# Up projection of a transformer block as seven products of quarters instead of eight, on one Trainium2 core

## What is computed

```python
xn2 = rmsnorm(x, norm2_g[l])
x = x + jnp.square(jax.nn.relu(xn2 @ w_up[l])) @ w_down[l]
```

## Time and profile before

| | |
|---|---|
| median of 3 runs | 1969.29 us |
| span of the profiled execution | 1967.4 us, 1.9 us less than the median |
| TensorE busy | 1959.2 us (100%), 9686 matmuls |
| VectorE busy | 1024.1 us (52%) |
| ScalarE busy | 764.9 us (39%) |
| GpSimd busy | 83.8 us, all after 1806 us |
| DMA | 183.36 MB, mean 93 GB/s, from the queues of SyncE and ScalarE |

### The profile page before, as it was taken

How to read it: one execution, slowest core, us unless ns; L and a number is a source line. 1 busy time by engine, 2 the same in 40 slices (tenths; PEclk the granted TensorE clock), 3 DMA queues, 4 the chain that set the end, 5 groups by cost and what they waited for, 6 DMA issues and landing times.

```text
span 1967.4 us, 23153 instructions
## 1 busy us (share of the span) xinstructions
PE 1959.2 (100%) x9686; PEld 1614.8 (82%) x9686; DVE 1024.1 (52%) x1394; ACT 764.9 (39%) x1226; POOL 83.8 (4%) x132
## 2 busy tenths in 40 slices
PE   9999999999999999999999999999999999999998
PEld 8888888888888888888888888888888888887776
DVE  5553466435453436643334355545554447596675
ACT  5556563332323333442134232222222321447864
POOL 0000000000000000000000000000000000005541
PEclk9999999999999999999999999999999999999999
DMA  6222222223122242233233323232323334521011
GB/s 214 84 68 85 65 86 75 86 91 106 65 91 86 87 148 86 86 107 108 86 105 89 106 86 107 86 107 89 105 86 107 86 124 114 152 81 44 23 55 65
DMA packets 184295, 183.36 MB, mean 93 GB/s; under 512 B 5120, under 2 KB 159232, under 8 KB 184192
## 3 DMA queue, kind: packets, MB, share of 16 engines
q1 hardware_dynamic: 179840, 172.15, 28.2%
q10 hardware_dynamic: 4352, 9.75, 1.6%
HBM read 175.59 MB, written 4.19 MB: 91 GB/s over the span
## 4 chain that ended last, share of the span: by engine, by line
PE 98%; ACT 1%; DVE 0%; DMA 0%; issue 0%; POOL 0%; DVEq 0%; ACTq 0%
PE bank L1403 85%; PE bank L1630 2%; PE bank L1611 2%; PE bank L1644 2%; PE bank L1501 1%; PE bank L1490 1%; PE bank L1529 1%; PE bank L1413 1%; ACT raw L1663 0%; PE bank L1464 0%; PE bank L1433 0%; PE bank L1509 0%; PE bank L1577 0%; PE bank L1446 0%; PE bank L1620 0%; PE bank L1431 0%
## 5 line engine op out<-in xcount | busy, mean ns | idle before, releaser
L1403 PE MATMUL bank<-xh,wh 128*128 128x512 f32 x1352 | 534.1, 395 | 0.0
L1403 PE MATMUL bank<-xh,wl 128*128 128x512 f32 x1352 | 527.6, 390 | 0.0
L1403 PE MATMUL bank<-xl,wh 128*128 128x512 f32 x1352 | 527.0, 390 | 0.0
L1680 ACT CAST wh<-raw 128x2048 fp32r<-128x2048 f32 (+2 forms) x151 | 279.5, 1854 | 408.8 <-PE bank L1403 405.1
L2234 DVE TENSOR_TENSOR wl<-raw,wh 128x2048 fp32r<-128x2048 f32 (+2 forms) x151 | 335.0, 2221 | 169.5 <-ACT wh L1680 169.3
L1403 PEld LDWEIGHTS bank<-xh,wl 128*128 128x128 f32 x1352 | 253.4, 187 | 53.8
L1403 PEld LDWEIGHTS bank<-xh,wh 128*128 128x128 f32 x1352 | 253.7, 188 | 50.3
L1403 PEld LDWEIGHTS bank<-xl,wh 128*128 128x128 f32 x1352 | 253.8, 188 | 50.0
L1403 PE MATMUL bank<-wh,xh 128*128 128x512 f32 x320 | 129.4, 404 | 0.0
L1403 PE MATMUL bank<-wh,xl 128*128 128x512 f32 x320 | 125.1, 391 | 0.0
L1403 PE MATMUL bank<-wl,xh 128*128 128x512 f32 x320 | 125.1, 391 | 0.0
(11 more groups left out here) (325 smaller groups left out, 2925.8 us busy)
## 6 DMA issues: line engine op xcount, KB each, us to landing
raw<-in_w_in SPq DMA_DIRECT2D x49, 1024.0 KB, 5.0
raw<-in_a_w_in SPq DMA_DIRECT2D x32, 1024.0 KB, 5.5
raw<-in_w_up SPq DMA_DIRECT2D x16, 1024.0 KB, 5.3
raw<-in_w_down SPq DMA_DIRECT2D x16, 1024.0 KB, 5.8
raw<-in_w_proj_b SPq DMA_DIRECT2D x8, 1024.0 KB, 5.1
raw<-in_a_w_out SPq DMA_DIRECT2D x8, 1024.0 KB, 5.7
raw<-in_w_out SPq DMA_DIRECT2D x4, 1024.0 KB, 5.2
raw<-in_w_kv SPq DMA_DIRECT2D x4, 1024.0 KB, 4.9
```

Source lines behind the costliest of these rows:

```text
L1403: m = e.matmul(o, p, q, start=k == 0 and n == 0, stop=k == K - 1 and n == 2)
L1680: m = e.copy(hi, r)
```

## The change

A group g of 512 columns of `w_up` within a half f is cut into quarters A, B, C and D of 512 x 256 (rows 0 to 511 are A and B, rows 512 to 1023 C and D; A and C are the first 256 columns). The tokens are cut into two times 256. In place of the eight products of quarters, seven are made, each of a sum of weights with a sum of x: A, A+B, A+B+D, A+B+D+C, B+D, C and D. One product is 24 matmuls with 256 columns moving (`seven`, three terms, two column blocks t, four k). There are 28 a half, in the sequence `SEVENS`, as pairs of group and number.

- Four of a group's products (1, 6, 5, 3) are accumulated into one bank. Three snapshots of it are copied to SBUF by ScalarE (`shot`, after 1, 6 and 5); the next product into the bank waits for the snapshot. Products 2, and 7 with 4, have banks of their own. VectorE adds or subtracts bank and snapshot and then applies maximum and `rs` (`piece`), piece 12 without the first step. ScalarE squares and rounds, VectorE makes the low part (`piece_low`, placed behind the next product).
- Each product has its own half slot (128 x 1024) of `wh`, `wl`, of which there are four; `part` splits the weights of the product four places on, on ScalarE and VectorE. In the list it stands behind the piece of the product that frees the slot.
- SyncE loads quarters of 512 KB into six half slots of `raw`. A+B is added in SBUF by VectorE (`add_weights`). A+B+D, A+B+D+C and B+D are made by DMAs issued from GpSimd that add a quarter from memory to the slot (`sum_weights`), after the low part of the product before is made.
- The sums of x (differences of the token halves and of the row halves) are made after each tile of `wo` by VectorE, in `between`, with high and low parts in `xh`, `xl` and new tiles `xeh`, `xel` of 768 columns a row.
- `ROOT[1]` is 2: the sum of squares and root come after the third product. `("up", 0, 2)` is no longer split in four pieces. Some semaphores are merged, `yh`, `yl` and others have new places in SBUF, a wait of `pa_low` is gone, and the indices of the splits in the last stretch are renumbered.

```diff
+SEVENS = [(0, 1), (1, 1), (0, 2), (0, 7), (0, 6), (1, 2), (0, 5), (1, 7), (0, 3), (0, 4),
+          (1, 6), (2, 1), (1, 5), (2, 2), (2, 7), (1, 3), (1, 4),
+          (2, 6), (3, 1), (2, 5), (3, 2), (3, 7), (3, 6), (2, 3), (3, 5), (2, 4), (3, 3), (3, 4)]
+SUM_OF = {1: ("A", 0), 7: ("A", 1), 6: ("A", 2), 3: ("A", 3), 5: ("B", 1), 2: ("C", 0), 4: ("D", 0)}
+PRODUCT_OF = {x: n for n, x in SUM_OF.items()}
+ADDED = {("A", 1): "B", ("A", 2): "D", ("A", 3): "C", ("B", 1): "D"}
+INTO = {1: "12", 6: "12", 5: "12", 3: "12", 2: "11", 7: "21", 4: "21"}
+SHOT = {1: "11", 6: "21", 5: "22"}
+X_PART = {1: 0, 5: 1, 2: 2, 3: 3, 7: 4, 6: 5, 4: 6}
+PIECE_OF = {2: "11", 5: "22", 3: "12", 4: "21"}
...
-            for j in range(2):
-                col(("up", f, c, j), ("up", f, c), j * 128, 8, ("x", 1), "out_d")
+        for x, g in QUARTER_LOADS:
+            chunk(("quarter", f, g, x), "w_up", 512 * (x in "CD"), 4, f * 2048 + g * 512 + 256 * (x in "BD"), 256,
+                  "quarter")
+        SPLIT.extend(("seven", f, g, n) for g, n in SEVENS)
...
+for _n, _c in enumerate(SPLIT):
+    _wide = 1 if _c[0] == "seven" else 2
+    WSLOT[_c] = _next // 2 if _wide == 2 else _next
+    _old = {_held[_next + x] for x in range(_wide)} - {None}
+    for x in range(_wide):
+        _held[_next + x] = _c
+    _next = (_next + _wide) % 4
+    if _old:
+        BEFORE[_c] = sorted(_old, key=SPLIT.index)
+        AFTER.setdefault(BEFORE[_c][-1], []).append(_c)
...
+def sum_ready(g, x, step):
+
+    at = SEVENS.index
+    return at((g, 5)) - 7 if x == "B" else at((g, PRODUCT_OF[x, step - 1])) - 3
+
+
+def sevens(f):
+
+    line = SEVENS
+    sums = sorted((sum_ready(g, x, step), g, x, step) for g in range(4) for x, step in ADDED if (x, step) != ("A", 1))
+    out, low = [], []
+    for i, (g, n) in enumerate(line):
+        while sums and (sums[0][0] <= i or i == len(line) - 1):
+            out.append(("sum_weights", f, *sums.pop(0)[1:]))
+        out.append(("seven", f, g, n))
+        if f == 0 and i == ROOT[1]:
+            out += [("sum_squares", 1), ("root", 1)]
+        if n in SHOT:
+            out.append(("shot", f, g, n))
+        if n in PIECE_OF:
+            out.append(("piece", f, g, PIECE_OF[n]))
+        out += low
+        for t in after_chunk(("seven", f, g, n)):
+            out += [t] + ([("add_weights", *t[1:3])] if t[0] == "part" and t[3] == 1 else [])
+        low = [("piece_low", f, g, PIECE_OF[n])] if n in PIECE_OF else []
+    return out + low
 
 
...
-        o += whole(("up", 1, 0, 0), ("up", 1, 0, 1)) if f else rooted(1, ("up", 0, 0, 0), ("up", 0, 0, 1))
-        o += whole(*[("up", f, c, j) for c in range(8) for j in range(2)][2:])
+        o += sevens(f)
...
+        def seven(f, g, n):
+            into = INTO[n]
+            if n in (1, 2, 7):
+                take("st" + into, ("st", f, g, into), ("st_out", f, g, into))
+            elif n == 4:
+                w.wait_ge(*told("st_out", f, g, "22"))
+            else:
+                w.wait_ge(*told("shot", f, g, {6: 1, 5: 6, 3: 5}[n]))
+            bank = bank_of("st" + into, ("st", f, g, into))
+            w.wait_ge(*told("lo", ("seven", f, g, n)))
+            hi, lo = split_half(("seven", f, g, n))
+            for t in range(2):
+                for k in range(4):
+                    w.wait_ge(*(told("xl", 1, k + 4, "sums") if X_PART[n] > 3 else told("xl", 1, k + 4 * (X_PART[n] > 1))))
+                    c = slice(k * 256 + t * 128, k * 256 + t * 128 + 128)
+                    h, l = x_sum(n, k)
+                    for x, (p, q) in enumerate(((hi, h), (hi, l), (lo, h))):
+                        m = e.matmul(bank[:, t * 256:(t + 1) * 256], p[:, c], q,
+                                     start=n in (1, 2, 7) and t == 0 and k == 0 and x == 0,
+                                     stop=t == 1 and k == 3 and x == 2, skip_group_check=True)
+            m.then_inc(*tell("tile", ("seven", f, g, n)))
+
...
+        def part(f, g, n):
+            name, (x, step) = ("seven", f, g, n), SUM_OF[n]
+            if (x, step) == ("A", 1):
+                w.wait_ge(*told("lo", "added", f, g))
+            elif step:
+                w.wait_ge(*told(f"sum{SUMS.index((f, g, x, step)) % 3}", f, g, x, step))
+            else:
+                w.wait_ge(*told(f"half{SLOT[PLACE['quarter', f, g, x]]}", f, g, x))
+            for old in BEFORE[name]:
+                w.wait_ge(*told(*chunk_read(old)))
+            e.copy(split_half(name)[0], raw_half(("quarter", f, g, x))).then_inc(*tell("hi", name))
+
+        def shot(f, g, n):
+            piece = SHOT[n]
+            w.wait_ge(*told("tile", ("seven", f, g, n)))
+            if piece_before(f, g, piece):
+                w.wait_ge(*told("hl", *piece_before(f, g, piece)))
+            elif piece == "11":
+                w.wait_ge(*told("xl", 1, 6 + g, "sums"))
+                w.wait_ge(*told("xl", 1, 6 + g))
+            elif piece == "21":
+                w.wait_ge(*told("sum_square", 1, 7))
+            else:
+                w.wait_ge(*told("ssq", 1))
+            e.copy(shot_place(g, piece)[:, :], bank_of("st12", ("st", f, g, "12"))[:, :]).then_inc(*tell("shot", f, g, n))
+
+        def piece(f, g, c):
+            t = shot_place(g, c)
+            w.wait_ge(*(told("st_out", f, g, c) if c == "12" else told("st_out", f, g, c, "relu")))
+            act(t[:, :], t[:, :], ACT.Square).then_inc(*tell("up_sq", f, g, c))
+            if f:
+                w.wait_ge(*told("tile", ("down", 0, 7, 0)))
+            else:
+                after("mix")
+            w.wait_ge(*told("up_sq", f, g, c))
+            e.copy(h_part(hh, g, c), two(t[:, :])).then_inc(*tell("hh", f, g, c))
...
         def wo(c, j):
-            gain(1, c * 2 + j, ("gb", 3, 1))
...
+            k = c * 2 + j
+            t, v = tmp[2 + k % 3], between[:, k % 2, :]
+            w.wait_ge(*told("tile", ("gb", 3, 1)))
+            w.wait_ge(*told("gain", 1, k))
+            if k < 4:
+                e.copy(xh[:, 2 * k, 0:256], t[:, 0:256]).then_inc(*tell("xh", 1, k))
+                w.wait_ge(*told("x_sum", k))
+                e.copy(xh[:, 2 * k, 256:512], v[:, 0:256]).then_inc(*tell("xh", 1, k, "sums"))
+            else:
+                e.copy(xh[:, 2 * k - 7, :], t[:, :]).then_inc(*tell("xh", 1, k))
+                w.wait_ge(*told("x_sum", k))
+                e.copy(xeh[:, k - 4, :], v[:, 0:768]).then_inc(*tell("xh", 1, k, "sums"))
...
+            if s == 1:
+                t, v = tmp[2 + k % 3], between[:, k % 2, :]
+                w.wait_ge(*told("xh", 1, k))
+                if k < 4:
+                    e.tensor_tensor(xl[:, 2 * k, 0:256], t[:, 0:256], xh[:, 2 * k, 0:256], ALU.subtract)
+                    w.wait_ge(*told("xh", 1, k, "sums"))
+                    e.tensor_tensor(xl[:, 2 * k, 256:512], v[:, 0:256], xh[:, 2 * k, 256:512], ALU.subtract).then_inc(
+                        *tell("xl", 1, k))
+                else:
+                    e.tensor_tensor(xl[:, 2 * k - 7, :], t[:, :], xh[:, 2 * k - 7, :], ALU.subtract).then_inc(*tell("xl", 1, k))
+                    w.wait_ge(*told("xh", 1, k, "sums"))
+                    e.tensor_tensor(xel[:, k - 4, :], v[:, 0:768], xeh[:, k - 4, :], ALU.subtract).then_inc(*tell("xl", 1, k, "sums"))
+                return
...
-            add_x(("wo", c, j), c * 2 + j, 1, "norm2_g")
+            k = c * 2 + j
+            t, v = tmp[2 + k % 3], between[:, k % 2, :]
+            add_x(("wo", c, j), k, 1, "norm2_g")
+            w.wait_ge(*told("gain", 1, k))
+            if k >= 2:
+                w.wait_ge(*(told("xl", 1, k - 2, "sums") if k >= 6 else told("xl", 1, k - 2)))
+            if k < 4:
+                e.tensor_tensor(v[:, 0:256], t[:, 0:256], t[:, 256:512], ALU.subtract).then_inc(*tell("x_sum", k))
+                if k == 0:
+                    e.tensor_scalar(minus_g, v_("norm2_g")[:, 0:4], -1.0, None, ALU.mult).then_inc(*tell("x_sum", "minus"))
+                return
+            stt(v[:, 0:256], xT[:, k - 4, 256:512], v_("norm2_g", k - 4), t[:, 256:512], ALU.mult, ALU.subtract).then_inc(
+                *tell("x_sum", k, "x_less"))
+            w.wait_ge(*told("x_sum", k, "x_less"))
+            w.wait_ge(*told("x_sum", "minus"))
+            stt(v[:, 256:512], xT[:, k - 4, 0:256], minus_g[:, k - 4:k - 3], v[:, 0:256], ALU.mult, ALU.add).then_inc(
+                *tell("x_sum", k, "x_least"))
+            w.wait_ge(*told("x_sum", k, "x_least"))
+            e.tensor_tensor(v[:, 512:768], t[:, 0:256], v[:, 256:512], ALU.add).then_inc(*tell("x_sum", k))
...
+        def part(f, g, n):
+            name = "seven", f, g, n
+            w.wait_ge(*told("hi", name))
+            hi, lo = split_half(name)
+            e.tensor_tensor(lo, raw_half(("quarter", f, g, SUM_OF[n][0])), hi, ALU.subtract).then_inc(*tell("lo", name))
+
+        def add_weights(f, g):
+            first, second = ("quarter", f, g, "A"), ("quarter", f, g, "B")
```

(41 more changed lines are left out.)

298 lines of the change are left out of this document (169 added, 129 removed).

## The result

The kernel after takes 2032.83 us (median of 4 runs, 2032.22 to 2034.21), the kernel before 1969.45 us beside it: a ratio of 1.0323, with a 95% interval of 1.0308 to 1.0337. That is 63.4 us slower. The forecast was 2021 us, 51.7 us slower, with a range of 1996 to 2056 us.

A forecast was written before the change was run, and what follows sets the result against it. TensorE bounds the kernel before; after, the VectorE-ScalarE chain was to limit the up stages. The four feed-forward stages were summed to 400 against 348.4 us, 51.5 more, added to the 1969.3 median: 2021 us, range 1996 to 2056.

The forecast's parts named there:

- The exchange of VectorE and ScalarE: Up stages: 4.83 us per piece with a part behind it, 24.8 us per group where TensorE needs 19.8.
- The sums: GpSimd's accumulating DMAs in the up stages: 7 us landing, each us lost four times, two places per half.
- TensorE's own work: Up stages: 174.2 us of products removed, 158.6 us of quarter products added; 15.6 us less if nothing else limited.
- Start and ends: Up stages: a 7.6 us stand at the first start; at each end the down split holds TensorE 3.8 us.
- The clock, taken at 0: TensorE's stands could lower its clock to 1.2 GHz: bounds 0 and 22 us, taken as 0.
- "Edits at no cost": Whole change: renamed and merged semaphores, missing pa_low wait, moved tiles, snapshots and load slots were said to cost nothing.
- nowhere else: Expected sign: TensorE waits some 50 us in the two up stages, for wl and the snapshot, and in no other place.
- Rival 1: Up stages: TensorE still limits, only the 15.6 us saving remains, 1954 us; chance 0.08.
- Rivals 2 and 3: Sums land in 3.4 us or less, 2006 us, chance 0.18; or take 10 to 12 us, chance 0.19.
- Rival 3: Up stages: sums take 10 to 12 us, by GpSimd's issue or DMA load, 2040 to 2060 us; chance 0.19.

The follow-up runs named there:

- fill: The kernel after with unread 128x256 matmuls put into TensorE's stands in the up stages, computation untouched: 2035.97 us (1.0337).
- best2: The kernel after with part rounding ahead of ScalarE's square and copy, another product order and banks moved back by two: 1969.10 us (0.9999).

## Why the prediction was right, and where it was off

The direction and the mechanism held: forecast 2021, measured 2032.8 us, 11.8 us more. Some 6 of these are the bank rotation and 5.4 the four stages. In part the nearness is luck: a sum was put at 7 us and lands in 6.0, which made the forecast 4 us too long and hid as much of what was put too short. With 6.0 the same sum of terms gives 2017. By its own steps:

- **The exchange of VectorE and ScalarE.** Right, and confirmed by taking it away (38.3 us). A piece with a part behind it takes 4.86 us for 4.83. The group of seven was put at 24.8 us; in after, products 5 of groups 1 and 2 are 26.2 us apart, in fill 24.8 in the first half and 25.8 in the second. TensorE's waits in the two up stages and at their ends add up to 48.4 us, for some 50.
- **The sums.** Landing 6.0 us (5.8 to 10.6) where 7 was taken; ScalarE stands 7.3, 7.5, 7.5 and 5.5 us in the four places, for about 8.2, and 2.1 in a fifth, behind a sum that took 8.0 us to land. Four places, 3.5 to 3.7 us per us of landing for 4. The reason given for 7, that the destination is read too and so the time doubles, was wrong in its size: the addition costs 1.7 us, and a plain load takes 4.3 from GpSimd and 3.8 from SP.
- **TensorE's own work.** The row gave 0.1175 us per matmul from four of them; in a full stage they start 0.12 apart, 80.6 us per half for 79.3. Of 174.2 us then 12.9 are saved and not 15.6, and best2's second half shows 4.5 of its 6.4.
- **Start and ends.** A stand of 8.6 us before the third product, for 7.6, ended by the low part of its weights in VectorE's late queue. Up stages of 121.6 and 106.9 us for 119.3 and 105.6, down stages of 88.1 and 88.8 for 87.5. In the last, nine of the first matmuls start late by 1.7 us in all, behind the stand at the hand-over.
- **The clock, taken at 0.** TensorE's clock did fall, in ten places of the two up stages, the granted mean being 0.90 and 0.92. The forecast's stages, 399.9 us, are 5.4 short of the 405.3; the 1.3 us of a group and the 1.7 us of the last stage fit the clock, but fill, with most of the slow matmuls gone, left the up stages as long as they were. What makes these 5 us stays open.
- **"Edits at no cost".** This is the step that failed. The list had renamed semaphores, moved tiles and slots. It did not have the ring of PSUM banks, from which the up stages no longer take 32 tiles. It costs 5.9 us, outside the two stages, where "nowhere else" had been written.
- **The rivals.** Rival 1 (TensorE limits, 1954) is what best2 comes near to in its second half; it needed another order on ScalarE, as its condition said, and still gained nothing in the whole: of the 4.5 us of the second half, 3.0 go in the first up stage, 1.0 in the down stage behind it and 0.8 ahead of the stages. Rivals 2 and 3 fell by the landing of 6.0 us. Rival 3's landings of 10 us exist, for the second of two sums in a row (9.8 to 10.6 us), but ScalarE stands for none of these in after. The load on the DMA engines, 0.64 of the time in a stage and 0.84 in best2's, did not keep best2's second half from its 82.4 us.

## What to carry to other kernels

When a change takes tiles out of a rotation (banks, slots, buffers), list every rotation by its count modulo its length, because all that comes later shifts; a shift shows as a new wait far from the edit, and moving the rotation on in the old kernel tests it in one run. When two in-order engines hand work to each other, put first on each queue what the other one waits for: here that alone was worth 38 us, more than the matrix work saved. A sum by DMA wants other products between the part that it waits for and the part that waits for it: one more product there cut ScalarE's waits from 29.9 to 4.8 us.

## What the runs showed of the hardware

An accumulating DMA of 512 KB from GpSimd lands in 6.0 us, the same without the addition in 4.3, one of 32 KB, accumulating, in 2.8; they hold GpSimd's queue for 1.28, 0.75 and 0.85 us. Of two accumulating ones in a row the second takes 9.8 to 10.6 us. VectorE and GpSimd, both on SBUF, stretch each other: 0.68 to 1.22 us and 0.49 to 1.04 us on VectorE, 0.72 to 1.22 on GpSimd. The Trainium skill, page "SBUF — State Buffer", section "Who interferes with whom", says that a VectorE instruction contends with a GpSimd instruction that reads SBUF if it has two SBUF inputs or is in a two-port mode, which a `tensor_scalar` can be, and that one with at most one SBUF input outside these modes does not. The trace agrees: the two-input addition and the `tensor_scalar` are stretched, and the addition from PSUM, 0.67 us, is the one that stays as it is. In which mode the `tensor_scalar` ran the trace does not show.
